# Output projection of an encoder layer as seven half-length block products, with the FFN gain folded into the router, gate and up weights

## The reference, cut to what matters

```python
h = rmsnorm(x, norm_mix_g)
proj = h @ w_in                                  # split into attention and mLSTM inputs
na_out = rmsnorm(neighbourhood_attention(...), na_norm_g)       # (1024, 1024)
ml_out = mlstm_mixer(...)                                       # (1024, 1024)
mix = concatenate([na_out, ml_out], axis=-1)                    # (1024, 2048)
x = x + mix @ w_out                                             # (1024, 2048) @ (2048, 2048)
h = rmsnorm(x, norm_ffn_g)
# each of 16 experts takes the 128 tokens of its highest router probability:
logits = h @ w_router                                           # (1024, 16)
gate, tok = top_k(softmax(logits).T, 128)
y = (silu(h[tok] @ w_gate) * (h[tok] @ w_up)) @ w_down          # per expert
x = x + scatter_add(y * gate at tok)
return rmsnorm(x, final_norm_g)
```

## Time and profile before

| what | value |
|---|---|
| median of 3 runs | 2692.42 us (2691.87 to 2692.95) |
| profiled execution, device time | 2693.19 us |
| its span, first to last instruction | 2691.4 us |
| mean granted clock of PE, share of full speed | 0.995 |
| DMA traffic | 827.49 MB, mean 307 GB/s |
| input projection, attention and mLSTM | 0 to 1153.6 us |
| output projection | 1153.6 to 1540.8 us |
| routing after it | 1540.8 to 1568.4 us |
| experts and last norm | from 1568.4 us |

### The profile page before, as it was taken

One profiled execution on the slowest core, in us unless ns is written; L12 is line 12 of the kernel. 1 busy time (PEld: TensorE's weight loads), 2 busy tenths in 40 slices (PEclk: granted clock), 3 DMA queues, 4 the chain that ended last, 5 costly groups with the idle time before them and its releaser, 6 DMA issues.

```text
span 2691.4 us, 33672 instructions
## 1 busy us (share of the span) xinstructions
PE 2649.8 (98%) x12357; PEld 2187.4 (81%) x12357; DVE 2067.9 (77%) x2578; ACT 1463.2 (54%) x1717; POOL 550.0 (20%) x805
## 2 busy tenths in 40 slices
PE   9999999999999999999999989999999999999996
PEld 7888888888888888788888878888888888888885
DVE  7775776487777666864357499999999999999887
ACT  6433221122232267843232368888888888888776
POOL 1422111211111244811010121111111111111002
PEclk9999999999999999999999999999999999999998
DMA  9688876898888766434453499999999999999998
GB/s 363 245 284 301 274 265 211 283 347 279 282 302 285 263 215 215 157 132 164 142 175 134 151 418 394 392 406 406 404 405 402 406 403 405 404 404 403 398 404 375
DMA packets 251044, 827.49 MB, mean 307 GB/s; under 512 B 30326, under 2 KB 55429, under 8 KB 227853
## 3 DMA queue, kind: packets, MB, share of 16 engines
q1 hardware_dynamic: 210528, 685.12, 67.2%
...
## 4 chain that ended last, share of the span: by engine, by line
PE 93%; DMA 1%; ACT 1%; DVE 1%; issue 1%; SPq 1%; POOL 0%; POOLq 0%; DVEq 0%; ACTq 0%
PE ps L3271 26%; PE ps L2900 6%; PE ps L2902 6%; PE ps L2901 6%; PE ps L2896 5%; PE ps L2897 5%; PE ps L2898 5%; PE ps L3116 4%; PE ps L3118 4%; PE ps L3117 4%; PE ps L3302 4%; PE ps L3301 4%; PE ps L3300 4%; PE ps L2951 1%; PE ps L3245 1%; PE ps L2839 1%
## 5 line engine op out<-in xcount | busy, mean ns | idle before, releaser
L2729 DVE TENSOR_TENSOR elo<-eraw,ehi 128x2048 fp32r<-128x2048 f32 x384 | 877.2, 2298 | 79.7 <-ACT ehi L1814 65.9
L1814 ACT ACTIVATE ehi<-eraw 128x2048 fp32r<-128x2048 f32 x384 | 733.3, 1920 | 215.4 <-PE ps L3271 133.3
L1442 ACT ACTIVATE whi<-raw 128x1024 fp32r<-128x1024 f32 x159 | 168.6, 1060 | 581.6 <-PE ps L2902 248.4
L3271 PE MATMUL ps<-ehi,xh 128*128 128x512 f32 x960 | 375.1, 391 | 0.0
L3271 PE MATMUL ps<-elo,xh 128*128 128x512 f32 x960 | 373.7, 389 | 0.0
L1932 DVE TENSOR_TENSOR wlo<-raw,whi 128x1024 fp32r<-128x1024 f32 x159 | 194.5, 1224 | 189.0 <-ACT whi L1442 188.6
L3271 PE MATMUL ps<-ehi,xl 128*128 128x512 f32 x960 | 256.6, 389 | 0.0
L3271 PEld LDWEIGHTS ps<-ehi,xl 128*128 128x128 f32 x960 | 180.2, 188 | 37.5
L3271 PEld LDWEIGHTS ps<-ehi,xh 128*128 128x128 f32 x960 | 180.2, 188 | 37.1
L3271 PEld LDWEIGHTS ps<-elo,xh 128*128 128x128 f32 x960 | 180.3, 188 | 36.9
L1700 ACT ACTIVATE ohi<-oraw 128x512 fp32r<-128x512 f32 x128 | 80.7, 631 | 237.9 <-PE ps L3118 237.8
...
## 6 DMA issues: line engine op xcount, KB each, us to landing
...
eraw<-in_w_gate SPq DMA_DIRECT2D x256, 512.0 KB, 8.0
eraw<-in_w_up SPq DMA_DIRECT2D x256, 512.0 KB, 10.1
eraw<-in_w_down SPq DMA_DIRECT2D x128, 1024.0 KB, 11.2
oraw<-in_w_stream SPq DMA_DIRECT2D x128, 256.0 KB, 2.6
xt<-in_xT SPq DMA_DIRECT2D x48, 256.0 KB, 4.2
scr_ops<-xt POOLq DMA_DIRECT2D x48, 256.0 KB, 3.3
nav<-scr_rows SPq DMA_DIRECT2D x128, 64.0 KB
```

The source lines that it names most:

```text
L1442: act.activation(whi[:, c % SPL, :], raw_pair(c)[0], ACT.Copy).then_inc(S["w_hi"], 1)
L1814: act.activation(ehi[:, p % ERING, :], flat2(eraw[:, 2 * (p % EDEEP):2 * (p % EDEEP) + 2, :]), ACT.Copy)\
L2729: dve.tensor_tensor(elo[:, p % ERING, :], flat2(eraw[:, 2 * (p % EDEEP):2 * (p % EDEEP) + 2, :]), ehi[:, p % ERING, :].bitcast(F32), ALU.s ...
L3271: last = pe.matmul(gu_bank(e, c), a[:, k, :], w[:, p % ERING, c * BW:(c + 1) * BW], start=(k == 0 and a is hi and w is ehi), stop=(k == KD ...
```

## The change

**Seven products.** Rows, inner dimension and columns are halved. Inner steps fall into K1 and K2 (8 each), rows into two groups of 512, and columns into pairs of 512-column blocks (pair 0: blocks 0 and 1, pair 1: blocks 2 and 3). For each column pair the four quarter products are formed from seven products instead of eight, after Strassen's scheme in Winograd's form. A product (index s = 0 to 13, type OTYPES[s // 2], pair s % 2) has 8 k-steps; there are NQO = 112 steps q. Four PSUM banks per product, by turns, as before.

**Sums of W.** Types p6 (s = 2, 3), p7, p4 and p5 (s = 4 to 9) multiply by a sum of quarters of W; p1, p3 and p2 by a quarter itself. SP fetches the quarters; DVE adds them in place (`w_combine`: two sums for p6, one for the three others). The p6 sum of each of 16 steps is stored to `w_sums` by a DMA that ACT issues, and p4 reloads it in place of two quarters. A slot is refilled only when its store has landed.

**Sums of mix.** The transposed `mix` is now kept whole in four quarters (`mix_f`, 64 tiles of 128x512 with their splits in `mix_r`). ACT writes a quarter's tile (`mix_out`), and for p1 its hi as well. Per type and k-step: `third_sum`, `first_second_sum` (DVE), `second_sum`, `op_summed` (POOL) form the left operands; `op_upper` (ACT) and `op_lower` (POOL) split them.

**Partial outputs.** A product adds to several output blocks. ACT copies products 0 and 1 into `run0` and `run1`; DVE adds them and x into outputs (`part_add`) and products 2 to 5 into the run buffers (`run_add`); `part_sum` (POOL), `run_part` and `run_ahead` (DVE) add run buffers to x or to stored parts. Unfinished blocks are stored to `x1` and fetched again (`store_part`, `fetch_x`, tables OSTEPS and XAT). Finished blocks leave with products 6 to 13, and transposes and logits lie in products 7 to 13.

**Nine lower halves on POOL.** In products 11 to 13 nine of the 24 `olo` are made by POOL (`out_lower`, table LOW_P). Rankings are spread over products 11 to 13 (RANKAT).

**The gain.** `out_gain` and `og` are gone. PE transposes the sum itself, `h2` holds it too. The gain is multiplied into the router weights (once, DVE), into `ehi` of gate and up (ACT's scale) and `elo` (a scalar_tensor_tensor on DVE in place of a tensor_tensor).

The core of the diff:

```diff
-KORD = [8, 9, 10, 11, 12, 13, 0, 1, 2, 3, 4, 5, 6, 7, 14, 15]
+K1, K2 = (8, 9, 10, 11, 12, 13, 0, 1), (2, 3, 4, 5, 6, 7, 14, 15)
+OTYPES = ("p1", "p6", "p7", "p4", "p5", "p3", "p2")
+OPARTS = {"p1": ((0, 0),), "p6": ((1, 1), (0, 1), (0, 0)), "p7": ((1, 1), (0, 1)), "p4": ((1, 0), None),
+          "p5": ((0, 1), (0, 0)), "p3": ((1, 1),), "p2": ((1, 0),)}
+LOW_P = [8 * s + k for s, ks in ((11, (5, 7)), (12, (1, 3, 5, 7)), (13, (1, 3, 5))) for k in ks]
...
             def fetch_out(q):
...
                 if q >= ORING:
-                    sp.wait_ge(S["w_lo"], NCH + q - ORING + 1)
+                    low_made(sp, q - ORING)
+                    if q - ORING in PARKED:
+                        sp.wait_ge(parksem[q % ORING], parked0[q % ORING] + 16 * (PARKED.index(q - ORING) // ORING + 1))
...
+                for part, at in enumerate(WPARTS[q]):
...
+                    sp.dma_start(w_raw(q, part), src).then_inc(rawsem[q % ORING], 16)
...
+            def op_lower(ty, i):
+
+                pool.wait_ge(S["op_high"], BEFORE["op_high"] + KO * (ty - 1) + i + 1)
+                pool.tensor_tensor(mix_low(ty, i), mix_whole(ty, i), mix_high(ty, i).bitcast(F32), ALU.subtract).then_inc(S["op_low"], 1)
...
                 act.activation(ohi[:, q % ORING, :], oraw[:, q % ORING, :], ACT.Copy).then_inc(S["w_hi"], 1)
+                if q in PARKED:
+                    act.dma_start(t["w_sums"][OPROD[q // KO][1], q % KO, :, :], oraw[:, q % ORING, :]).then_inc(parksem[q % ORING], 16)
...
+            def w_combine(q):
...
+                dve.tensor_tensor(a, a, w_raw(q, 1), ALU.subtract).then_inc(S["o_sum"], 1)
+                if WSUM[q] == 2:
...
+                    dve.tensor_tensor(a, a, w_raw(q, 2), ALU.add).then_inc(S["o_sum"], 1)
...
+            for q in range(ORING, NQO):
+                if q not in LOW_P:
+                    out_low(q)
+                if q + 1 < NQO:
+                    w_combine(q + 1)
...
+                if kind == "gu":
+                    dve.scalar_tensor_tensor(out=elo[:, p % ERING, :], in0=raw_, scalar=mixg[:, k:k + 1],
+                                             in1=ehi[:, p % ERING, :].bitcast(F32), op0=ALU.mult, op1=ALU.subtract).then_inc(S["e_lo"], 1)
```

More of the change, by code:

```diff
@@ new lines, in out_lower, with part_sum @@
+            def out_lower(q):
+                pool.wait_ge(S["w_hi"], NCH + q + 1)
+                pool.tensor_tensor(olo[:, q % ORING, :], oraw[:, q % ORING, :], ohi[:, q % ORING, :].bitcast(F32), ALU.subtract)\
+                    .then_inc(S["w_low_p"], 1)
+            def part_sum(n):
+                pool.wait_ge(oxinsem[OSTEPS[n][4]], xin0[OSTEPS[n][4]] + 16 * x_loads(n))
+                for j in range(4):
+                    a = oxs[:, OSTEPS[n][4], j, :]
+                    pool.wait_ge(S["o_run"], BEFORE["o_run"] + 4 * (n - 2) + j + 1)
+                    pool.tensor_tensor(a, run[n % 2][:, j, :], a, ALU.add).then_inc(S["o_part_p"], 1)
@@ L1329, in _ @@
+            store_final(4)
+            for q in LOW_P[:3]:
+                out_lower(q)
+            store_final(5)
+            for q in LOW_P[3:7]:
+                out_lower(q)
+            store_final(6)
+            for q in LOW_P[7:]:
+                out_lower(q)
+            store_final(7)
+            row_scales_of(1)
             place_columns()
```

665 lines of the change are left out of this document (433 added, 232 removed), and 3 rows, old and new, of the table OSTEPS.

## The result

The changed kernel takes 2709.04 us (2708.37 to 2710.96, 4 runs), the one before 2692.14 us (2691.4 to 2692.95, 4 runs). The ratio is 1.0064 with a 95% interval of 1.0046 to 1.0081: slower, where 2664 us had been forecast. The span of the profiled execution is 2706.6 us for 2691.4, so 15.2 us more.

What follows compares the result with a forecast made beforehand. PE was taken to bound the output projection. From the profiled 2693.2 us, -43.5 - 0.7 + 12 + 3 + 1 = -28.2 gave 2665.0, and the runs' median, 0.8 lower, 2664 us; range 2649 to 2684.

Steps and rivals of the forecast that it cites:

- The removal: Output projection: 1,344 product matmuls instead of 1,536, so 16 k-steps of 2.72 us go, -43.5 us.
- The gain at the end: End of the output projection: the last transposes start after the sum, without the ffn gain's multiplication, -0.7 us.
- The experts: Experts' gate and up: elo as scalar_tensor_tensor costs DVE 12.8 us, mostly covered by the ring of pairs, +1 us.
- The weight ring: Products 2 and 3: slot refills just fit, with nothing over; with an x block wait in product 6, +3 us.
- The turn of 10.1 to 10.8 us: Products 2 and 3: one slot's split, store, loads and sums, to fit in four PE steps of 10.9 us.
- DVE and POOL: Output projection: DVE and POOL largely exclude each other, so PE stalls, in products 5 and 6 and at later borders, +12 us.
- a wait for lgT: Start of product 8: PE waits until DVE has taken the block's logits from the bank, 3.1 us.
- the 6.4 us of slack: Output projection: how far DVE may lag before the four-slot ring of split weights no longer hides it.
- The strict exclusion: Output projection: DVE and POOL exclude each other for whole instructions, the upper bound of +39 us; chance 0.06.
- nothing is left: Rival for the output projection: stalls of 39 to 50 us, time 2687 to 2698 us; chance 0.06.
- POOL decides: Slower rival: loss from 1.70 us per POOL operation with handover, 2722 us at 2.0; PE waits on mix_r; chance 0.10.
- What was to show it: Output projection of 350 to 370 us; PE waiting for olo in products 5 and 6; sums well over 0.69 us beside POOL.

Runs made afterwards that it cites:

- e1: The changed kernel with POOL's elementwise work for products 1 to 10 moved to DVE; 2675.03 us.
- e2: The changed kernel without the 16 stores of the p6 sums and the waits for them, so p4's weights are not the right ones; 2700.0 us.
- e3: The changed kernel with both edits, POOL's work for products 1 to 10 on DVE and no stores of the p6 sums; 2663.1 us.
- e4: The changed kernel with the experts' gate and up weights split without the gain; 2711.45 us.
- e7: The changed kernel with each of POOL's eight type 5 op_summed waiting for one more lower half of DVE; 2700.58 us.
- e11: The kernel before plus 24 unused POOL operations in blocks 5 and 6, each waiting for one more lower half of DVE; 2692.8 us.
- e9: e1 with second and third weight quarters fetched ahead of the waits, x blocks moved, and six of them cut into four loads each; 2663.23 us.

## Why the prediction was wrong, point by point

The time came out 45 us above the forecast of 2664. Products 2 to 9 hold 59 us of stall where the prediction had 15. The runs divide them so: POOL's work 34.0 us (e1), the stores 9.0 (e2), 2.9 more when both are gone (e3), and 13 that e3 still has: 5.0 in product 4, where SP stands before an x block, 3.0 of clock in product 5, 1.8 in product 7, the rest in small pieces.

- **The removal.** -43.5 us was right: product 1 takes 21.76 us in every changed kernel, 8 steps of 2.72.
- **The gain at the end, -0.7 us.** It is not there. From the projection's last matmul with `olo` to the first gate and up matmul it is 29.9 us before (1540.19 to 1570.07) and 30.2 after (1554.56 to 1584.72).
- **The experts, +1 us.** Gate and up last 1045.7 us from first to last start before and 1045.2 after, so nothing of the 1 us shows; e4 shows no cost that its runs could tell. The operation's own price was right.
- **The weight ring, +3 us.** This term was too small: e2 says 9.0, products 2 and 3 alone 8.2. Two numbers of the step failed. It took 406 GB/s for the DMA from the experts' stage, but the window of this very stage shows 148 GB/s at a share of 0.43, which is 344 at full share, and e3 shows 346 at 0.97 and 356 at 1.01: 21.0 MB take 59 to 61 us and not 52. And it took landing times from a stage with a half idle DMA: the store took 5.3 us for the 3.0 to 3.5 counted, the third quarter 6.0. The turn of 10.1 to 10.8 us, with nothing over, had no room for that.
- **DVE and POOL, +12 us.** This is the step that turned the sign: with POOL's work on DVE the kernel is 34 us faster. It also had the places wrong: it put 7.2 us into products 5 and 6 and none before them, but products 3 and 4 have 19.5 us of stall (part of them the ring's) and 5 and 6 have 16.5. At the start of product 8 it expected a wait for lgT of which 0.22 us came; the stall of product 8 is the long piece. The price of one meeting was right: a DVE and a POOL operation in turn were to take 0.60 + 1.14 = 1.74 us and take 1.78. What failed is how they were put together, in three ways. First, the step added up DVE's operations as a full queue that never idles once it is late. But `w_combine` runs one step ahead only: DVE waits for ACT's split, ACT for DVE's sum. A sum that is held up holds up this loop, and the 0.70 us of idle time in each step is not usable: 3.09 us a step where the count gave room. In e1 an operation that came from POOL fills this gap, and the step's three operations take 2.0 us (1322.54 to 1324.53). Second, POOL was taken to come in single operations. It comes in pieces of four and eight, and DVE's turn comes after the piece: 10.94 us, more than the 6.4 us of slack that the step gave the ring, where the pieces of four cost PE 2.44 us of idle time (product 9), 0.99 (e7) or none (e11). Third, each stall costs again in clock: the granted clock was 0.89 to 0.94 in six of the eight products above, and of the 58.5 us some 19 lie inside PE's busy time. The prediction had no term for it.
- **The rivals.** The strict exclusion, which I had given 39 us at most and a chance of 0.06 as "nothing is left", bounded an exclusion per instruction. The runs show one that lasts over several instructions. The rival "POOL decides" (0.10) had the right sign and the right pair of engines, but not the mechanism: it needed 1.70 us for each POOL operation with its handover, and the loss came by idle time in DVE's loop and by waits behind whole pieces. Its sign, PE waiting on mix_r from POOL, showed in two weight loads alone, 3.6 us together in products 2 to 9. The range ended at 2684 us because I let POOL's share grow only by such a price.
- **What was to show it.** An `olo` and sums of W well over 0.69 us beside POOL were named as signs, though nothing like 10.94 us, as was PE waiting in products 5 and 6. PE waiting in products 2 and 3 was named as the sign that the ring fails, and it was there as well.

Not settled: how much of the stall that is left in products 2 and 3 of e9 (7.9 us) is the DMA's rate and how much the turn of the slot; what part of e1's 34 us is exclusion itself and what part the new order; and why DVE gets its turn after each POOL operation at some places (1268.83) and after the last only at others (1394.32). In the long cases seen DVE's operation began while POOL was still issuing its stores (1393.89, 0.43 us before POOL's first operation) or in POOL's first operation, but so did some of the short ones. No run separates these.
